# Eleven pairs of expert tiles by seven block products in the second half of V

## The chip, the cores and the metric

The kernel runs on one core of a Trainium2 chip. The metric is the device time of one launch in microseconds. A core has TensorE for matmuls, VectorE, ScalarE and GpSimd for elementwise work, and DMA queues; here SyncE (SP) issues nearly all transfers.

## The reference

Two transformer blocks on 256 tokens of width 2048, all in float32. The change touches the last matmul only. After the second block's attention, each token chooses experts out of 16384. With `u` and `v` the tables of the chosen experts:

```python
a = jax.nn.gelu(jnp.einsum('thkd,td->thk', u, xb).astype(jnp.float32), approximate=False)
coef = (g * a).astype(xb.dtype)
return jnp.einsum('thk,thkd->td', coef, v_emb[expert])
```

The result is added to `x`, and an RMS norm with the gain `norm_final_g` gives the output.

## The kernel before

All experts are computed densely. `G[expert, token]` (128 expert tiles of 128, by 256 tokens) holds the coefficients, zero where a token didn't choose an expert, and the V stage computes `G`-transposed times V (16384 by 2048). It runs in two halves of 1024 columns, c = 0 and c = 1. In each half, tile j adds for two token halves (qt) and two column blocks of 512 (b) a product of 128 x 128 by 128 x 512 to one of four PSUM banks (`acc`, line 832). Float32 accuracy is kept with two parts of each operand, a high part rounded to fp32r and the low rest, so each product is three matmuls (`three`, lines 940 to 943: high by high, high by low, low by high). A tile is 12 matmuls.

`PLAN` is the list of all weight chunks in order of use (512 KB each here), `AT` its inverse, `NCH` its length. Each engine runs its own program in that order:

- SP loads chunk i to one of RN = 4 places of `raw` (`load`, line 838), once VectorE is done with chunk i - 4 (semaphore `lo`). What stands in front of a load on SP holds it back.
- ScalarE casts chunk i to `wh` (line 2273), after its load has landed (`d_w`) and after TensorE finished chunk i - SN, SN = 3 (`gemm`). VectorE writes `wl` = `raw` - `wh` (line 1481) and signals `lo`.
- `coef_high(n)` (line 2655, ScalarE) and `coef_low(n)` (line 2189, VectorE, semaphore `c_l`) do the same for the coefficients of tile n mod 128, in two places used by turns. `coef_high(n)` waits until TensorE finished tile n - 2.
- In the loops over j for the second half, ScalarE and VectorE do the coefficients of tile j + 1 and then the weights of tile j + 2. ScalarE's turn j starts when TensorE has finished tile j - 1.
- TensorE (`v_tile`) waits for `lo` and `c_l` of its tile.

Around this: the residual (`spill`, 8 pieces of 256 KB) and the final gain (4 pieces) are read back into `G`'s own space while the second half runs. `PIECE` says at which chunk, and each piece n waits on SP for `c_l` >= 128 + 2n + 2, since it overwrites the coefficients of used tiles. `ADD_AT` says in which turns VectorE adds the first half's four PSUM banks to the residual. ScalarE squares the sums with an accumulated row sum, and VectorE multiplies by the gain, a little later. The last three tiles are ordered by bank (`v_last`), so that the final norm can begin early. GpSimd has no work after the placing of the weights in the table.

```python
PIECE = {AT["V", 10 + 2 * n, 1]: n for n in range(12)}
ADD_AT = [50 + 4 * n for n in range(4)]
```

Of the kernel before, what the change touches and what calls it, by code (L numbers as in the profile page):

```python
# [7 lines left out]
F32 = mybir.dt.float32  # L8
# [8 lines left out]
D = 2048  # L17
# [143 lines left out]
PLAN += [("V", j, c) for c in range(2) for j in range(128)]  # L161
# [7 lines left out]
PIECE = {AT["V", 10 + 2 * n, 1]: n for n in range(12)}  # L169

ADD_AT = [50 + 4 * n for n in range(4)]
# [323 lines left out]
def build(nc, A, out):  # L495
# [184 lines left out]
    fin = flatG[:, 0:2 * D].rearrange("p (q d) -> p q d", q=2)  # L680
# [26 lines left out]
    def pc(name, i=0):  # L707
# [53 lines left out]
        new(n) for n in ("v_part", "f_add", "f_sq", "f_ms", "f_rt", "f_rs", "f_out", "f_outv")]  # L761
    block = top.enter_context(nc.Block())
# [74 lines left out]
    def _(y):  # L837
# [42 lines left out]
        for i in range(RN, NCH):  # L880
# [30 lines left out]
            if i in PIECE:  # L911
                n = PIECE[i]
                if n == 0:
                    y.wait_ge(d_spill, 16)
                y.wait_ge(c_l, 128 + 2 * n + 2)
                c = slice(512 * (n % 4), 512 * (n % 4) + 512)
                if n < 8:
                    y.dma_start(fin[:, n // 4, c], spill[:, n // 4, c]).then_inc(d_re, 16)
                else:
                    y.dma_start(gain[:, c], A["g_final"][:, c]).then_inc(d_gf, 16)  # L920
            load(i)
# [6 lines left out]
        for qt in range(2):  # L928
            for n in range(2):
                for sem, c in ((f_out, 512 * n), (f_outv, CH + 512 * n)):  # L930
                    if (qt, n, sem) == (1, 1, f_out):
                        continue
                    y.wait_ge(sem, 2 * qt + n + 1)
                    y.dma_start(out[128 * qt:128 * qt + 128, c:c + 512], fin[:, qt, c:c + 512]).then_inc(d_out, 16)
# [4 lines left out]
    def _(t):  # L939
# [495 lines left out]

        def v_last():
# [16 lines left out]
        for i in range(U0, NCH):  # L1453
            name, j, c = PLAN[i]
            if name == "U":
                if c == 0:
                    if j < 4:
                        t.wait_ge(qp_ok, 5 + j)
                    else:
                        t.wait_ge(ev_u, j - 3)  # L1460
                chunk(i, u_place(j), 8 * c, 8, x4, c == 0, c == 1)
            elif (j, c) == (125, 1):
                v_last()
            elif c == 0 or j < 125:
                v_tile(j, c)
# [6 lines left out]
    def _(v):  # L1472
# [731 lines left out]
        def add_up(half, qt, b):  # L2204
            i = 2 * half + b
            x = fin[:, qt, 512 * i:512 * i + 512]
            v.tensor_tensor(x, x, acc(half, qt, b)[:], ALU.add).then_inc(f_add, 1)

        for j in range(128):
            if j < 125:  # L2210
                coef_low(128 + j + 1)
# [11 lines left out]
            else:  # L2223
                cut(V1 + j + 2)
            if j in ADD_AT:
                n = ADD_AT.index(j)
                if n == 0:
                    v.wait_ge(d_re, 16 * 8)
                add_up(0, n // 2, n % 2)
            if j - 2 in ADD_AT:  # L2230
                n = ADD_AT.index(j - 2)
                if n == 0:
                    v.wait_ge(d_gf, 16 * 4)
                x = fin[:, n // 2, 512 * (n % 2):512 * (n % 2) + 512]
                v.wait_ge(f_sq, n + 1)
                v.tensor_tensor(x, x, gain[:, 512 * (n % 2):512 * (n % 2) + 512], ALU.mult).then_inc(own.up(), 1)
        for qt in range(2):
            for b in range(2):
# [6 lines left out]
                else:  # L2245
                    for c in (0, 256):
                        x = fin[:, 1, 1536 + c:1792 + c]
# [9 lines left out]
            for c in (CH, CH + 512):  # L2257
                y = fin[:, qt, c:c + 512]
# [4 lines left out]
    def _(s):  # L2263
# [404 lines left out]
        def square_up(half, qt, b):  # L2668
            i, n = 2 * half + b, 4 * half + 2 * qt + b
            s.wait_ge(f_add, n + 1)  # L2670
            s.activation(squares[:, qt, 512 * i:512 * i + 512], fin[:, qt, 512 * i:512 * i + 512], ACT.Square,
                         accum_out=ssum[:, qt, i:i + 1]).then_inc(f_sq, 1)

        for j in range(128):
            if j < 126:
                coef_high(128 + j + 1)
# [8 lines left out]
            else:  # L2685
                cut(AT["V", j, 1] + 2)
            if j - 1 in ADD_AT:
                n = ADD_AT.index(j - 1)
                square_up(0, n // 2, n % 2)
        for qt in range(2):  # L2690
# [4 lines left out]
            else:  # L2695
                for n, c in ((0, 1536), (1, 1792)):
                    s.wait_ge(f_add, 8 + n)
                    s.activation(squares[:, 1, c:c + 256], fin[:, 1, c:c + 256], ACT.Square,
# [14 lines left out]
    def _(g):  # L2713
# [91 lines left out]
        put(1, 7)  # L2805

# [118 lines left out]
```

## Time and profile before

| What | Value |
| --- | --- |
| median of 3 runs | 3174.89 us (3174.85 to 3175.99) |
| profiled execution | 3175.95 us, of it 3174.1 us span |
| mean granted TensorE clock | 0.999 |
| TensorE matmuls | 24186 |
| second half of V | about 2812 to 3161 us |

The span runs from the first to the last instruction. "Busy" of TensorE counts pipelined matmuls: one lasts 0.39 us in the records but the next begins 0.23 us after it, so the pitch, not the duration, gives its cost. A line of the profile names line, engine, operation, output and inputs. The tile `coefs` is the pair of coefficient buffers, and `G` also stands for everything laid over its space.

### The profile page before, as it was taken

What the parts mean: (1) busy time and instruction counts of PE and PEld (TensorE: products, weight loads), DVE (VectorE), ACT (ScalarE), POOL (GpSimd) and SP (SyncE); (2) the same over time, 40 slices, a digit from 0 to 9 for tenths busy, and PEclk for the clock granted to TensorE, in tenths of its full rate; (3) what the DMA queues carried; (4) which work ended last, traced back from release to release, by engine and by line L of the source; (5) the groups of instructions that cost most, each with busy time, mean ns of one, the idle gap of its engine ahead of it and who ended that gap; (6) DMA issues with size and microseconds to landing.
All of it is one profiled execution on the core that took longest, in us unless ns stands there. A gap on an engine that the chain in (4) does not pass through costs nothing.

```text
span 3174.1 us, 58774 instructions
## 1 busy us (share of the span) xinstructions
PE 3160.3 (100%) x24186; PEld 3018.3 (95%) x24186; DVE 2096.0 (66%) x3389; ACT 1804.0 (57%) x2580; POOL 458.0 (14%) x321
## 2 busy tenths in 40 slices
PE   9999999999999999999999999999999999999998
PEld 9999999999999999999999999999999888888887
DVE  7987486666664477665666699855555666666665
ACT  6566464444444455545455578877777544555545
POOL 0001200000000000000000056777760000000000
PEclk9999999999999999999999999999999999999999
DMA  6444557666666656545565577888876777766555
GB/s 224 151 146 134 183 181 235 225 226 229 226 201 194 194 172 206 163 153 166 187 196 197 199 190 194 196 195 195 194 195 196 243 242 242 242 226 216 195 194 168
DMA packets 229419, 627.77 MB, mean 198 GB/s; under 512 B 59328, under 2 KB 78624, under 8 KB 229024
## 3 DMA queue, kind: packets, MB, share of 16 engines
q1 hardware_dynamic: 192144, 623.60, 60.7%
q0 software_dynamic: 36864, 0.15, 3.3%
q8 instruction: 192, 3.15, 0.4%
q14 instruction: 75, 0.61, 0.1%
q10 hardware_dynamic: 144, 0.26, 0.0%
HBM read 601.27 MB, written 21.10 MB: 196 GB/s over the span
## 4 chain that ended last, share of the span: by engine, by line
PE 98%; DVE 1%; ACT 0%; DMA 0%; issue 0%; POOL 0%; SPq 0%; DVEq 0%; ACTq 0%; POOLq 0%
PE ps L941 32%; PE ps L942 31%; PE ps L943 31%; PE ps L1014 0%; DVE wl L1481 0%; PE ps L1215 0%; PE ps L1238 0%; PE ps L1235 0%; PE ps L982 0%; DMA raw<-in_in1k 0%; PE ps L1411 0%; PE ps L1249 0%; PE ps L1239 0%; PE ps L1067 0%; PE ps L1016 0%
## 5 line engine op out<-in xcount | busy, mean ns | idle before, releaser
L2273 ACT CAST wh<-raw 128x1024 fp32r<-128x1024 f32 (+3 forms) x1114 | 1158.2, 1040 | 1029.7 <-PE ps L943 1008.4
L1481 DVE TENSOR_TENSOR wl<-raw,wh 128x1024 fp32r<-128x1024 f32 (+2 forms) x883 | 1061.8, 1203 | 407.8 <-ACT wh L2273 405.4
L941 PE MATMUL ps<-xh,wh 128*128 128x256 f32 x3088 | 854.7, 277 | 0.5 <-issue 0.5
L943 PE MATMUL ps<-xh,wl 128*128 128x256 f32 x3088 | 850.0, 275 | 0.0
L942 PE MATMUL ps<-xl,wh 128*128 128x256 f32 x3088 | 849.8, 275 | 0.0
L941 PE MATMUL ps<-xw,wh 128*128 128x258 f32 (+2 forms) x2096 | 591.7, 282 | 2.8 <-DVE wl L1542 1.7
L943 PE MATMUL ps<-xw,wl 128*128 128x258 f32 (+2 forms) x2096 | 587.6, 280 | 0.0
L941 PEld LDWEIGHTS ps<-xh,wh 128*128 128x128 f32 x3088 | 579.7, 188 | 4.3 <-issue 1.6
L942 PEld LDWEIGHTS ps<-xl,wh 128*128 128x128 f32 x3088 | 579.8, 188 | 1.1 <-issue 1.0
L943 PEld LDWEIGHTS ps<-xh,wl 128*128 128x128 f32 x3088 | 579.6, 188 | 0.0
L2784 POOL DMA_INDIRECT table<-w_loose x256 | 397.6, 1553 | 809.3 <-DVE w_loose L2161 656.3
L1481 DVE TENSOR_TENSOR wl<-raw,ph 128x1024 fp32r<-128x1024 f32 x231 | 281.2, 1220 | 224.4 <-ACT ph L2278 187.7
L942 PE MATMUL ps<-xw,wh 128*128 128x258 f32 (+2 forms) x1441 | 404.2, 281 | 0.0
L941 PEld LDWEIGHTS ps<-xw,wh 128*128 128x128 f32 x2096 | 394.3, 188 | 5.4 <-DVE wl L1542 2.1
L943 PE MATMUL ps<-wh,coefs 128*128 128x512 f32 x1020 | 396.8, 389 | 0.0
L941 PE MATMUL ps<-wh,coefs 128*128 128x512 f32 x1020 | 396.8, 389 | 0.0
L942 PE MATMUL ps<-wl,coefs 128*128 128x512 f32 x1020 | 396.8, 389 | 0.0
L943 PEld LDWEIGHTS ps<-xw,wl 128*128 128x128 f32 x2096 | 394.0, 188 | 0.0
L942 PEld LDWEIGHTS ps<-xw,wh 128*128 128x128 f32 x1441 | 270.8, 188 | 0.1
L2278 ACT CAST ph<-raw 128x1024 fp32r<-128x1024 f32 x231 | 232.7, 1007 | 0.0
L941 PEld LDWEIGHTS ps<-wh,coefs 128*128 128x128 f32 x1020 | 191.4, 188 | 39.8
L943 PEld LDWEIGHTS ps<-wh,coefs 128*128 128x128 f32 x1020 | 191.4, 188 | 39.8
(398 smaller groups left out, 4454.7 us busy)
## 6 DMA issues: line engine op xcount, KB each, us to landing
raw<-in_peer_u SPq DMA_DIRECT2D x256, 512.0 KB
raw<-in_peer_v SPq DMA_DIRECT2D x256, 512.0 KB
raw<-in_w_in SPq DMA_DIRECT2D x172, 512.0 KB
raw<-in_w_up SPq DMA_DIRECT2D x82, 512.0 KB
raw<-in_w_gate SPq DMA_DIRECT2D x80, 512.0 KB
raw<-in_w_down SPq DMA_DIRECT2D x80, 512.0 KB
raw<-in_w_out SPq DMA_DIRECT2D x64, 512.0 KB
table<-tmp SPq DMA_DIRECT2D x32, 512.0 KB, 6.4
```

Of the source, the lines that this page charges most:

```text
L941: t.matmul(o, lh, rh, start=start, stop=False)
L942: t.matmul(o, lh, rl, start=False, stop=False)
L943: return t.matmul(o, ll, rh, start=False, stop=stop)
L1481: v.tensor_tensor(part_at(wl, i), raw[:, i % RN, 0:cols(i)], high.bitcast(F32), ALU.subtract).then_inc(lo, 1)
L2273: last = s.copy(part_at(wh, i), raw[:, i % RN, 0:cols(i)])
L2278: last = s.copy(ph[:, 2 + i % 2, :], raw[:, i % RN, 0:cols(i)])
L2784: g.indirect_dma_start(out=table, out_offset=bass.IndirectOffsetOnAxis(ap=eidx[q][:, n:n + 1], axis=0), in_=wts[q][:, n:n + 1], in_offset= ...
```

## The change

Eleven pairs of neighbouring tiles (26 and 27, 34 and 35, ..., 106 and 107) leave the ordinary order of the second half. For such a pair the eight block products (two tiles, two token halves, two column blocks) are replaced by seven, in the manner of Strassen and Winograd, with four sums of weight blocks (T1 to T4) and four sums of coefficient blocks.

- TensorE: `v_pair(n)` runs ahead of the tile behind the pair, 7 x 3 matmuls. Three products go to the banks of the second half, four to the banks `ps[4]` to `ps[7]` of the first half, which are kept over all pairs.
- SP: the pair's raw weights (2 x 512 KB) go to a place of their own in `G`'s space (`PAIR_LOAD`). They stand ahead of the load of the chunk eight places behind the first single tile of the stretch, and wait for the fourth of the previous pair's five subtractions (`pair_lo`).
- GpSimd: `pair_sums`, 4 subtractions of 512 columns and 4 ops of 128 columns a pair, after TensorE has finished the previous pair (the sums lie where the low parts will).
- ScalarE and VectorE: `pair_step`, the cast and the subtraction of the pair's 4096 columns in five parts, one a turn in the six turns between two pairs, behind the turn's own work (VectorE one turn after ScalarE).
- Behind the last pair VectorE folds the four extra banks into the residual (`FOLD`, eight ops in turns 109 to 116), ScalarE copies one bank.
- `PIECE`, `ADD_AT`, the squares and the gains move: residual pieces 0 to 3 to tiles 8 to 14, 4 to 7 to tiles 109 to 112, the gain to tiles 18 to 24; the waits for `c_l` stay as they were.

```diff
-PLAN += [("V", j, c) for c in range(2) for j in range(128)]
+PAIRS = [26 + 8 * n for n in range(11)]
+PAIRED = [j + e for j in PAIRS for e in range(2)]
+SINGLE = [j for j in range(128) if j not in PAIRED]
+PLAN += [("V", j, 0) for j in range(128)] + [("V", j, 1) for j in SINGLE]
...
-PIECE = {AT["V", 10 + 2 * n, 1]: n for n in range(12)}
-
-ADD_AT = [50 + 4 * n for n in range(4)]
+PIECE = {AT["V", j, 1]: n for n, j in enumerate((8, 10, 12, 14, 109, 110, 111, 112, 18, 20, 22, 24))}
+
+ADD_AT = [11, 12, 13, 14]
+SQUARE_AT, GAIN_AT = [48, 56, 64, 72], [49, 57, 65, 73]
...
+BETWEEN = PAIRS[1] - PAIRS[0] - 2
+PAIR_LOAD = {AT["V", 20, 1]: 0}
+PAIR_LOAD.update({AT["V", j - BETWEEN, 1] + 8: n + 1 for n, j in enumerate(PAIRS[:-1])})
+BEHIND_PAIR = {j - BETWEEN + o: (n, o) for n, j in enumerate(PAIRS) for o in range(BETWEEN)}
+FOLD = {PAIRS[-1] + 3 + n: n for n in range(8)}
...
                 y.wait_ge(c_l, 128 + 2 * n + 2)
                 c = slice(512 * (n % 4), 512 * (n % 4) + 512)
+                if n == 4:
+                    y.wait_ge(pair_lo, PAIR_LO + 5 * (len(PAIRS) - 1) + 4)
...
+            if i in PAIR_LOAD:
+                n = PAIR_LOAD[i]
+                if n:
+                    y.wait_ge(pair_lo, PAIR_LO + 5 * (n - 1) + 4)
+                else:
+                    y.wait_ge(c_l, 128 + 16)
+                for e in range(2):
+                    j = PAIRS[n] + e
+                    y.dma_start(flatG[:, (2 + e) * CH:(3 + e) * CH], A["peer_v_2"][128 * j:128 * j + 128, CH:2 * CH]).then_inc(d_pair, 16)
             load(i)
...
+            if first:
+                t.wait_ge(f_add, 4)
+            t.wait_ge(pair_lo, PAIR_LO + 5 * (n + 1))
+            t.wait_ge(c_l, one + 1)
+            product(ps[4], single(one, 0), B11, first, last)
+            product(ps[5], summed(0), T1_, first, last)
+            t.wait_ge(c_l, two + 1)
+            product(acc(1, 0, 0), single(two, 0), B21, False, False)
+            product(acc(1, 1, 0), single(two, 1), T4_, False, False).then_inc(pair_mm, 1)
+            product(acc(1, 0, 1), summed(3), B22, False, False)
+            product(ps[6], summed(1), T2_, first, last)
+            product(ps[7], summed(2), T3_, first, last).then_inc(pair_mm, 1)
...
+        def pair_step(n, o):
+            if 1 <= o < 6:
+                pair_low_of(n, o - 1)
+
+        def pair_low_of(n, q):
+            x, y = ((0, 512), (512, 1536), (1536, 2560), (2560, 3584), (3584, 4096))[q]
+            whole_ = RAW11 if q == 0 else RAW_ROWS if q == 1 else pair_raw[:, x:y]
+            v.wait_ge(pair_hi, PAIR_HI + 5 * n + q + 1)
+            v.tensor_tensor(pair_low[:, x:y], whole_, pair_high[:, x:y].bitcast(F32), ALU.subtract).then_inc(pair_lo, 1)
...
+            if j in PAIRS:
+                coef_low(128 + j + 1)
+                cut(AT["V", j + 2, 1] + 2)
+                continue
...
+            elif n >= 130 and n - 130 in PAIRED:
+                s.wait_ge(pair_mm, PAIR_MM + 2 * (PAIRED.index(n - 130) // 2) + 1)
...
+            if o == 0:
+                if n:
+                    s.wait_ge(pair_mm, PAIR_MM + 2 * n)
+                s.wait_ge(d_pair, D_PAIR + 32 * (n + 1))
+            elif o > 1:
+                s.wait_ge(pair_sum, PAIR_SUM + 8 * n + (3, 4, 8)[o - 2])
+            s.copy(pair_high[:, x:y], whole_).then_inc(pair_hi, 1)
...
+            if n:
+                g.wait_ge(pair_mm, PAIR_MM + 2 * n)
+            g.wait_ge(d_pair, D_PAIR + 32 * (n + 1))
+            g.tensor_tensor(t1, RAW12, RAW11, ALU.subtract).then_inc(pair_sum, 1)
+            g.tensor_tensor(t3, RAW22, RAW12, ALU.subtract).then_inc(pair_sum, 1)
```

## Rows read from the trace of the kernel before

**Rows 1.** The page: engine, busy us, share of the span, instructions.

```profile
PE 3160.3 (100%) x24186; PEld 3018.3 (95%) x24186; DVE 2096.0 (66%) x3389; ACT 1804.0 (57%) x2580; POOL 458.0 (14%) x321
```

**Rows 2.** The page: the chain that ended last, by engine.

```profile
PE 98%; DVE 1%; ACT 0%; DMA 0%; issue 0%; POOL 0%; SPq 0%; DVEq 0%; ACTq 0%; POOLq 0%
```

**Rows 3.** Waits, 2812 to 3160: who waited for whom; total us, times, longest.

```profile
ACT coefs L2655 <- PE ps L943: 168.3, 126, 1.4
DVE wl L1481 <- ACT wh L2273: 66.1, 125, 0.6
```

**Rows 4.** Timeline of one tile: start, duration, engine, line, operation [idle before it].

```profile
2841.90 0.39 PE L941 MATMUL ps<-wh,coefs 128*128 128x512 f32 x1
...
2842.10 0.41 ACT L2655 CAST coefs<-G 128x256 fp32r<-128x256 f32 x1 [1.36 <-PE ps L943]
...
2842.41 1.05 ACT L2273 CAST wh<-raw 128x1024 fp32r<-128x1024 f32 x1
2842.54 0.42 DVE L2189 TENSOR_TENSOR coefs<-G,coefs 128x256 fp32r<-128x256 f32 x1 [0.54 <-ACT coefs L2655]
...
2843.50 1.22 DVE L1481 TENSOR_TENSOR wl<-raw,wh 128x1024 fp32r<-128x1024 f32 x1 [0.53 <-ACT wh L2273]
...
2844.62 0.39 PE L941 MATMUL ps<-wh,coefs 128*128 128x512 f32 x1
```

**Rows 5.** Timeline, VectorE in the first half of V, ops back to back.

```profile
2802.74 0.42 DVE L2189 TENSOR_TENSOR coefs<-G,coefs 128x256 fp32r<-128x256 f32 x1 [0.82 <-ACT coefs L2655]
2803.09 1.22 DVE L1481 TENSOR_TENSOR wl<-raw,wh 128x1024 fp32r<-128x1024 f32 x1
2804.22 0.42 DVE L2185 TENSOR_TENSOR G<-G,tmp 128x256 f32<-128x256 f32 x1
```

**Rows 6.** Groups by form, 2812 to 3160: VectorE on 512 columns.

```profile
L2220 DVE TENSOR_TENSOR wl<-raw,wh 128x512 fp32r<-128x512 f32 x2 | 1.3, 687 | 0.1
```

**Rows 7.** Timeline of SP's queue, 2839 to 2845: start, duration of the issue.

```profile
2839.31 0.33 SPq L842 DMA_DIRECT2D raw<-in_peer_v  x1
2839.68 0.43 SPq L918 DMA_DIRECT2D G<-spill  x1
```

**Rows 8.** DMA issues (whole run; last line 2850 to 3160): count, KB, us to landing.

```profile
spill<-G SPq DMA_DIRECT2D x1, 2048.0 KB, 7.8
...
par<-in_par SPq DMA_DIRECT2D x1, 8.0 KB, 1.7
...
G<-spill SPq DMA_DIRECT2D x4, 256.0 KB, 5.4
```

**Rows 9.** Windows: us, busy of PE, PEld, DVE, ACT, POOL; clock, DMA share, GB/s.

```profile
3165.00:3166.00 1.00, 0.94 (x5) 0.42 (x3) 1.00 (x2) 0.50 (x2) 0.00 (x0) 1.00 0.31 119
3166.00:3167.00 1.00, 0.00 (x0) 0.00 (x0) 0.74 (x3) 0.88 (x3) 0.00 (x0) 1.00 1.03 387
3168.00:3169.00 1.00, 0.00 (x0) 0.00 (x0) 0.70 (x3) 0.72 (x2) 0.00 (x0) 0.66 0.55 191
3169.00:3170.00 1.00, 0.00 (x0) 0.00 (x0) 0.90 (x2) 0.82 (x2) 0.00 (x0) 0.50 0.00 0
```

**Rows 10.** Timelines of GpSimd beside VectorE; last, line 1648: min/median/max ns.

```profile
931.34 0.74 POOL L2721 TENSOR_TENSOR tmp<-tmp 128x256 f32<-128x256 f32 x1 [481.18 <-ACT tmp L2437]
...
114.74 1.21 DVE L1481 TENSOR_TENSOR wl<-raw,wh 128x1024 fp32r<-128x1024 f32 x1
114.90 1.65 POOL L2759 TENSOR_TENSOR csum<-cacc 128x258 f32<-128x258 f32 x1 [88.48 <-DVE cacc L1692]
...
115.87 0.71 DVE L1648 SCALAR_TENSOR_TENSOR pexp<-pexp,stat 16x16 f32<-16x16 f32 x1
...
L1648 DVE SCALAR_TENSOR_TENSOR pexp<-pexp,stat x12: 217/350/706, 115.9 to 184.8; 16x16 f32<-16x16 f32 x4, 128x144 f32<-128x144 f32 x4, 128x272 f32<-128x272 f32 x4
```

More of the change, by code:

```diff
@@ L1434, in v_tile, with v_pair, product, single @@
             last.then_inc(gemm, 1)
+        def v_pair(n):
+            j = PAIRS[n]
+            one, two = 128 + j, 128 + j + 1
+            first, last = n == 0, n == len(PAIRS) - 1
+            def product(o, left, b, start, stop):
+                return three(o[:], *left, pair_block(pair_high, b), pair_block(pair_low, b), start, stop)
+            def single(tile, qt):
+                tk = slice(128 * qt, 128 * qt + 128)
+                return coef_at(0, tile)[:, tk], coef_at(1, tile)[:, tk]
+            def summed(i):
+                return pair_sum_at(pair_high, i), pair_sum_at(pair_low, i)
+            if first:
[10 more added lines that the diff above has]
+            product(ps[7], summed(2), T3_, first, last).then_inc(pair_mm, 1)
         def v_last():
@@ L1464, in _ @@
             elif c == 0 or j < 125:
+                if c and j - 2 in PAIRS:
+                    v_pair(PAIRS.index(j - 2))
                 v_tile(j, c)
@@ L2222, in _ @@
                 last.then_inc(lo, 1)
-            else:
-                cut(V1 + j + 2)
+            elif j in SINGLE and j - 2 not in PAIRS:
+                cut(AT["V", j, 1] + 2)
+            if j in BEHIND_PAIR:
+                pair_step(*BEHIND_PAIR[j])
+            if j in FOLD:
+                fold(FOLD[j])
             if j in ADD_AT:
@@ L2684, in _ @@
                 s.copy(part_at(wh, i)[:, 512:CH], raw[:, i % RN, 512:CH]).then_inc(hi, 1)
-            else:
+            elif j in SINGLE and j - 2 not in PAIRS:
                 cut(AT["V", j, 1] + 2)
-            if j - 1 in ADD_AT:
-                n = ADD_AT.index(j - 1)
+            if j in BEHIND_PAIR:
+                pair_step(*BEHIND_PAIR[j])
+            if j == PAIRS[-1] + 2:
+                s.wait_ge(pair_mm, PAIR_MM + 2 * len(PAIRS))
+                s.copy(folded, ps[6][:]).then_inc(pair_hi, 1)
+            if j in SQUARE_AT:
+                n = SQUARE_AT.index(j)
                 square_up(0, n // 2, n % 2)
@@ L2805, in _, with pair_sums @@
         put(1, 7)
+        def pair_sums(n):
+            j = PAIRS[n]
+            g.wait_ge(coef, j + 2)
+            g.wait_ge(c_l, 128 + 16)
+            a11, a21, a12, a22 = [G[:, j + e, 128 * qt:128 * qt + 128] for e in range(2) for qt in range(2)]
+            t1, t2, t3, t4 = [pair_block(pair_raw, b) for b in (T1_, T2_, T3_, T4_)]
+            sums = [pair_sum_at(pair_raw, i) for i in range(4)]
+            done = PAIR_SUM + 8 * n
+            if n:
[3 more added lines that the diff above has]
+            g.tensor_tensor(t3, RAW22, RAW12, ALU.subtract).then_inc(pair_sum, 1)
+            g.wait_ge(pair_sum, done + 1)
+            g.tensor_tensor(t2, RAW22, t1, ALU.subtract).then_inc(pair_sum, 1)
+            g.wait_ge(pair_sum, done + 3)
+            g.tensor_tensor(t4, RAW21, t2, ALU.subtract).then_inc(pair_sum, 1)
+            g.tensor_tensor(sums[0], a21, a22, ALU.add).then_inc(pair_sum, 1)
+            g.tensor_tensor(sums[2], a11, a21, ALU.subtract).then_inc(pair_sum, 1)
+            g.wait_ge(pair_sum, done + 5)
+            g.tensor_tensor(sums[1], sums[0], a11, ALU.subtract).then_inc(pair_sum, 1)
+            g.wait_ge(pair_sum, done + 7)
+            g.tensor_tensor(sums[3], a12, sums[1], ALU.subtract).then_inc(pair_sum, 1)
+        for n in range(len(PAIRS)):
+            pair_sums(n)
     px.close()
```

62 lines of the change are left out of this document (48 added, 14 removed).

## The prediction

> **What bounds the kernel now.** I read the page from the top: TensorE is busy for the whole span, VectorE and ScalarE for two thirds or less [rows 1]. The chain of waits says the same: 98% of the path that ended last is TensorE [rows 2]. So the time is the number of matmuls times their pitch, plus each pause in them. The changed stage is the second half of V (about 2812 to 3160 us). Its waits show that the other engines wait for TensorE: ScalarE 168 us at the coefficients, VectorE 66 us for ScalarE [rows 3]; TensorE waits for nobody. One tile tells the schedule [rows 4]: its first matmul starts at 2841.90, the next tile's at 2844.62, so a tile is 2.72 us for 12 matmuls of 512 columns, 0.227 each. I call a tile's start S. In loop turn j ScalarE casts the coefficients of tile j+1 at S+0.20 and the weights of tile j+2 at S+0.51; VectorE subtracts the coefficients at S+0.64 to 1.06 and the weights at S+1.60 to 2.82. The coefficients are 1.66 us ahead of their use, the weights 2.6 us. Both engines work through their queue in order: a wait in front of one cast holds everything behind it.
>
> Busy ops follow each other faster than they last [rows 5]: VectorE 1.13 us for 1024 columns, 0.35 for 256. 512 columns last 0.69 us [rows 6]; for their pitch I take 0.60.
>
> **What is saved.** A pair of tiles has 8 block products of 3 matmuls, now 7: 3 x 0.227 = 0.68 us a pair, 7.5 us for eleven. That is 0.24% and the most the change can bring. U, the first half of V and the tail stay.
>
> **Added work.** Per pair ScalarE and VectorE each go over 4096 columns instead of 2048. VectorE in turn j of a working tile: 0.35 + 1.13 + 1.13 = 2.6 us of 2.72. It fits, but only just, and it comes late: the pair's subtraction stands behind the tile's, at S+2.73 to 3.96. The eight folds (j = 109 to 116) and the moved additions, squares and gains are one short op in a turn that has at least 0.4 us left: nothing, the tile's 2.72 us cover them.
>
> **Pair start.** The last of the five subtractions (512 columns of sums) is in turn PAIRS-1, after the weights: 2.73 to 3.42 after S, while TensorE wants it at 2.72. `v_pair` waits for all five, so it starts 0.70 us late, 0.75 with the wake-up. What is queued behind is all of TensorE. This alone eats the 0.68. Where GpSimd has delayed VectorE before (below), it is up to 1.7, most of one GpSimd op more. I take 1.0, near the lower end, since only the last turns count (bounds 0.75 and 1.7; not below, because VectorE's own queue makes the 0.75).
>
> **Pair loads on SP's queue.** `PAIR_LOAD` for pair n+1 stands in front of the load of the fifth single tile behind pair n's beginning: for pair 26 it is tile 30. SP first waits for the fourth subtraction of pair n (call its end W: turn 24, S+3.96, that is 1.5 us before the pair is due), then issues 2 x 512 KB, and only then the 512 KB of tile 30. ScalarE wants tile 30 in turn 26, as the pair begins, ahead of the cast of tile 28's coefficients. How long do 1536 KB take? No row has it. SP's issues are 0.37 us apart [rows 7]. A 256 KB piece issued 0.37 behind a 512 KB load lands after 5.4 us, so 768 KB after 5.8 from the first issue; the 2048 KB spill takes 7.8 [rows 8]. Between them on a straight line: 1536 KB 7.0 us, 1792 KB 7.4. Lower bound: the 1.7 us of the 8 KB transfer [rows 8] plus the bytes at the 387 GB/s that the engines moved at the end [rows 9]: 5.8 us, and 3.7 for 768 KB, 6.4 for 1792. I take the line, because it lies between two landings of this very queue.
> So tile 30 lands at W+7.05. The pair starts at W+2.25 and ends at W+2.25+21 x 0.227 = W+7.0. From a landing to the next tile's first matmul: ScalarE's cast 1.05, VectorE's subtraction 1.13, then the coefficients 0.42, wake-ups 0.2: 2.8 us. TensorE stands for about 2.85 us behind each pair but the last.
>
> **GpSimd's sums.** They wait for the pair's end, so GpSimd starts just then. Alone, 256 columns took 0.74 us; behind a subtraction of VectorE (114.74 to 115.95) 1.65 us, 0.60 after that ended; and VectorE's next op, a 16x16 one of 0.22 at least, took 0.71 [rows 10]. So the two take turns, and a waiting GpSimd gets its turn between two VectorE ops. For 512 columns I take a little over twice the 0.60: 1.25 us. One such op ahead of the subtraction (which hides about 0.5 of it) or one between it and the coefficients adds 0 to 2.0 us to the 2.85. I take 1.25, one op in the way: 4.1 in all (bounds 2.85 and 4.85).
> The Trainium skill ("SBUF — State Buffer", Who interferes with whom) states this as an exclusive lock between a VectorE op with two SBUF inputs and a GpSimd op, held for the whole instruction; the rows agree (1.65 against 0.74). It speaks against "GpSimd makes the sums" being free. Without it the sum would be 12 us lower.
> Per pair: -0.68 + 1.0 + 4.1 = +4.4; ten pairs +44 us.
>
> **Last pair.** No pair load follows, but piece 4 (in front of tile 109) waits for the same fourth subtraction, then 256 KB, then tile 109: 768 KB from 1.5 before the due start, so landing 4.35 after it. ScalarE wants it in turn 105, and VectorE's last subtraction for the pair stands behind it: 1.05 + 1.13 + 0.69 + 0.1. The pair starts 7.3 us late. -0.68 + 7.3 = +6.6.
>
> **Moved pieces of the gain.** Pieces 8 to 11 move from tiles 26 to 32 to tiles 18 to 24, but their wait (c_l >= 146, 148, 150, 152) is unchanged: it is met in turns 16, 18, 20, 22. The load of tile 18 is behind it on SP, and ScalarE wants tile 18 in turn 16. Before, the same wait was long met. Tile 18: 1.1 (coefficients of turn 16) + 5.8 + 2.8 = 9.7 for the 5.44 of two tiles: +4.3. Tile 20: the wait is met 1.45 after tile 18's start; pair 0's 1024 KB go ahead too, 7.4; +2.8 = 11.65: +6.2. Tile 22: 1.45 + 5.8 + 2.8: +4.6. Tile 24: pair 0's subtractions add 0.6 before and 1.1 behind, 11.75: +6.3. Sum +21.4 us; with the fast transfers 7.3 less, +14.1.
>
> **Sum.** 21.4 + 44 + 6.6 = +72.0 us on the profiled execution's 3175.95: 3248; it is 1.06 above the median of the runs, so 3247.
> The Trainium skill ("DMA: Bandwidth & Descriptors", Anatomy of one DMA) fits one transfer with about 2.0 us plus bytes over 436 GB/s: 5.6 us for 1536 KB, 3.8 for 768. By that estimate the sum would be 23 us lower. The rows for queued transfers (5.4 and 7.8) are slower, and no row has one load alone.
>
> **Rivals.**
> A, fast transfers: landings by the lower bound. Pieces 14.1, pair waits 2.85 - 1.2 = 1.65 with GpSimd hidden: ten pairs x 2.0 = 20, the last 6.6 - 2.1 = 4.5: +38.6, so 3214 - 1 = 3213. With the 0.75 at the pair starts too it is 3211. For it: 387 GB/s in the end's row. Against it: both landings of SP's queue.
> B, TensorE's clock falls in the pauses. TensorE ended at about 3165.9; the granted clock was 1.00 until 3167, 0.66 in the mean of 3168 to 3169 and 0.50 (the 1.2 GHz level) after that [rows 9]. The fifteen pauses forecast here are 4 to 7 us long. No row shows it coming back; if each pause costs one tile at the half level, that is 2.72 more, so 0 to 41 us on top. The middle of that gives 3268. The Trainium skill ("TensorE: Matmul & The Clock Gate", Part 1) says that activity releases the throttle again, so it would be a price per pause. Against it: later stalls shrink while TensorE is slow.
> C, the other side, faster: the preparation never binds and only the 7 products count. Then 3174.9 - 7.5 = 3167.4. It decides where the fourth subtraction is over 5 us earlier, or the queue delivers 1536 KB in under 4 us, and where the 0.70 of the last subtraction vanishes; the first two I see nowhere.
> D, only the pair start binds (SP's waits are met early): -7.5 + 11 x 0.85 = +2, 3177. For it: SP's queue is empty when it wakes. Against it: the 5.8 us.
> E, the change doesn't do what it says: a pair in fact keeps its eighth product and the time stays. `v_pair` lists seven, so I give it nothing.
>
> **How the numbers follow.** Forecast with its own spread 0.50, A 0.20, B 0.20, C 0.04, D 0.06. Range 3205 to 3285: the low end is A less one microsecond at every second pause, the high end B with most of its price. A measurement tells 0.2% (6.3 us) from no change. Faster: C, 0.04. Same: D, 0.06. Slower: 0.90.
>
> **What would show it.** Matmuls down by 33. TensorE waiting for VectorE's coefficient subtraction at tiles 18, 20, 22, 24 (4 to 6 us each) and at the tile behind each pair (about 4), with ScalarE's weight cast waiting for the DMA `raw`; a wait of 0.7 to 1.7 at each pair start, over 7 before the last. GpSimd's 512-column ops 1.2 us alone and 2 to 2.5 behind VectorE. If ScalarE's cast never waits for `raw`, the sum is wrong from its base, and it is C or D. If the granted clock drops under 1 in the stage, B.

## The result: 3276.4 us, 3.2% slower, and the profile after

The changed kernel takes 3276.43 us in the median of 4 runs (3274.3 to 3278.46), the kernel before 3174.88. The ratio is 1.0319, with a 95% interval of 1.0301 to 1.0337. The time is 29 us above the forecast of 3247 and inside its range of 3205 to 3285.

The page of the kernel after: busy us of each engine, the granted clock in 40 slices of the span (9 is 90% or more), and the chain that ended last.

```profile
span 3274.2 us, 58871 instructions
...
PE 3192.3 (97%) x24153; PEld 3030.7 (93%) x24153; DVE 2148.7 (66%) x3430; ACT 1824.6 (56%) x2614; POOL 548.0 (17%) x409
...
PEclk9999999999999999999999999999999999989899
...
PE 91%; DVE 4%; DMA 3%; ACT 1%; issue 0%; SPq 0%; POOL 0%; DVEq 0%; ACTq 0%; POOLq 0%
```

The 33 matmuls are saved (24186 before [rows 1]). But the chain, 98% TensorE before [rows 2], now has 4% of VectorE and 3% of DMA in it, and the clock has dents in the last slices. The waits of the second half of V (2808 to 3262; us in total, times, longest), beside [rows 3]:

```profile
ACT coefs L2758 <- PE ps L984: 159.1, 96, 7.9
DVE wl L1552 <- ACT wh L2374: 116.0, 69, 8.9
ACT wh L2374 <- DMA raw<-in_peer_v: 87.7, 16, 9.3
...
PE ps L982 <- DVE coefs L2260: 56.2, 14, 6.2
```

Two lines are new: ScalarE's weight cast waits 16 times for a load, and TensorE 14 times for coefficients. Fourteen is four pieces of the gain and ten pairs.

**A piece of the gain** (timeline: start, duration, engine, line [idle before]; tile 18 was due at about 2865.5):

```profile
2861.14 0.33 SPq L952 DMA_DIRECT2D G<-in_g_final  x1
...
2861.51 0.91 SPq L871 DMA_DIRECT2D raw<-in_peer_v  x2
...
2867.17 1.04 ACT L2374 CAST wh<-raw 128x1024 fp32r<-128x1024 f32 x1 [6.51 <-DMA raw<-in_peer_v]
2868.12 0.40 ACT L2758 CAST coefs<-G 128x256 fp32r<-128x256 f32 x1
2868.24 1.22 DVE L1552 TENSOR_TENSOR wl<-raw,wh 128x1024 fp32r<-128x1024 f32 x1 [7.13 <-ACT wh L2374]
...
2869.95 0.77 PE L982 MATMUL ps<-wh,coefs 128*128 128x512 f32 x1 [4.30 <-DVE coefs L2260]
```

The piece is issued at 2861.14, the tile's load behind it, and the cast begins at 2867.17: 6.0 us for 768 KB, forecast 5.8. From there to the matmul it is 2.78, forecast 2.8.

**Behind a pair** (timeline; the pair's last matmul is the first line):

```profile
3028.70 0.39 PE L984 MATMUL ps<-xh,xl 128*128 128x512 f32 x1
3029.33 1.27 POOL L2943 TENSOR_TENSOR x_loose<-G 128x512 f32<-128x512 f32 x1 [20.27 <-PE ps L984]
3029.84 1.83 DVE L1552 TENSOR_TENSOR wl<-raw,wh 128x1024 fp32r<-128x1024 f32 x1 [4.99 <-ACT wh L2374]
3030.55 2.24 POOL L2944 TENSOR_TENSOR x_loose<-G 128x512 f32<-128x512 f32 x1
3031.60 2.89 DVE L2260 TENSOR_TENSOR coefs<-G,coefs 128x256 fp32r<-128x256 f32 x2
...
3033.22 0.76 PE L982 MATMUL ps<-wh,coefs 128*128 128x512 f32 x1 [4.13 <-DVE coefs L2260]
```

VectorE's subtraction, 1.22 us alone, lasts 1.83 behind GpSimd's first op; GpSimd's second, 1.27 alone, lasts 2.24 behind VectorE; the two subtractions of coefficients take 2.89 with a GpSimd op between them, 0.42 each alone [rows 4].

**Where the 101 us are.** I took the start of every 512-column matmul from the timeline and sorted the distances to the next one against 0.2267 us, the spacing of before [rows 4]. Over 0.35 us too long is a pause; 0.1 to 0.35 too long is a slow matmul; the rest is spacing. In after there are 140 slow ones, 114 of them 0.42 to 0.43 us apart. From "all three mended" on, the clock is 1.00 in the whole stage, so there the column holds short waits and no slow clock. Against it stand the 33 matmuls that are gone, 7.5 us. The last column is the time of the profiled execution less the before of its chip (3174.8 to 3175.2). The kernels below the first line are those of the experiments.

| kernel | pauses | slow matmuls | longer spacing | saved | sum | measured |
| --- | --- | --- | --- | --- | --- | --- |
| after | 73.3 | 27.8 | 7.5 | -7.5 | 101.1 | 101.1 |
| gain's pieces later | 59.9 | 23.9 | 5.4 | -7.5 | 81.7 | 82.2 |
| pair load later | 37.7 | 13.0 | 8.5 | -7.5 | 51.7 | 52.6 |
| GpSimd later | 57.8 | 24.3 | 7.9 | -7.5 | 82.5 | 82.5 |
| fillers, short | 74.1 | 14.6 | 7.2 | -7.5 | 88.4 | 88.0 |
| fillers, long | 76.8 | 4.1 | 8.4 | -7.5 | 81.8 | 82.0 |
| all three mended | 12.6 | 4.3 | 8.6 | -7.5 | 18.0 | 18.4 |
| and the sums first | 2.7 | 4.5 | 9.7 | -7.5 | 9.4 | 10.0 |
| mended, thin sums | 7.6 | 1.1 | 7.7 | -7.5 | 8.9 | 9.3 |
| before, one wait added | 1.2 | 0.0 | 8.9 | 0 | 10.1 | 9.6 |
| thin sums, sums first | 0.0 | 0.5 | 7.7 | -7.5 | 0.7 | 0.6 |
| VectorE makes the sums | 0.4 | 0.6 | 8.0 | -7.5 | 1.5 | 2.3 |
| and products in halves | 0.0 | 0.8 | 8.7 | -7.5 | 2.0 | 1.4 |

The sum closes to within 1 us in every kernel, so three things, and no fourth, have to be explained: pauses (forecast), slow matmuls (a rival), and a longer spacing (in nobody's forecast).

The slow matmuls are TensorE's clock. Windows of after (us; busy of PE, PEld, DVE, ACT, POOL; granted clock, DMA share, GB/s) over a pause that ends at 2946.50:

```profile
2944.00:2946.50 2.50, 0.00 (x0) 0.03 (x1) 2.50 (x3) 0.00 (x0) 2.50 (x2) 1.00 0.60 234
...
2946.50:2948.00 1.50, 1.50 (x5) 1.21 (x6) 1.27 (x1) 0.00 (x0) 1.42 (x2) 0.67 0.75 273
2948.00:2950.00 2.00, 2.00 (x6) 1.58 (x5) 0.00 (x0) 0.00 (x0) 2.00 (x4) 0.50 0.03 10
2950.00:2951.00 1.00, 1.00 (x5) 0.79 (x4) 0.00 (x0) 0.00 (x0) 0.60 (x2) 0.78 0.00 0
2951.00:2952.00 1.00, 1.00 (x6) 0.82 (x5) 0.42 (x1) 0.88 (x2) 0.00 (x0) 1.00 0.00 0
```

In this pause the clock is still 1.00. It falls to 0.50, the 1.2 GHz level, when TensorE works again, and is back at 1.00 by 2951. Elsewhere it falls within the pause, as in the one above that ends at 3033.22:

```profile
3032.40:3033.20 0.80, 0.00 (x0) 0.01 (x1) 0.80 (x2) 0.00 (x0) 0.80 (x2) 0.50 0.37 113
```

It fell thirteen times in the stage, nine times within a pause and four times up to 0.9 us behind one. Either way it stays low for some microseconds in which TensorE works again, so the price of a pause is paid by the matmuls behind it.

### The profile page after: what moved, and what is told of

The parts are those of the page before. It is cut to its first block, busy times and chain, and to the rows that moved or that the text cites. A ratio compares the mean times of both kernels' runs of the same rounds, so it can differ in the third digit from the quotient of the medians.

```text
span 3274.2 us, 58871 instructions
## 1 busy us (share of the span) xinstructions
PE 3192.3 (97%) x24153; PEld 3030.7 (93%) x24153; DVE 2148.7 (66%) x3430; ACT 1824.6 (56%) x2614; POOL 548.0 (17%) x409
## 4 chain that ended last, share of the span: by engine, by line
PE 91%; DVE 4%; DMA 3%; ACT 1%; issue 0%; SPq 0%; POOL 0%; DVEq 0%; ACTq 0%; POOLq 0%
PE ps L982 29%; PE ps L983 29%; PE ps L984 29%; DMA raw<-in_peer_v 3%; DVE wl L1552 2%; ACT wh L2374 1%; DVE xl L2288 1%; DVE coefs L2260 1%; PE ps L1055 0%; SPq L961 0%; DMA raw<-in_in1k 0%; PE ps L1256 0%; PE ps L1276 0%; PE ps L1279 0%; PE ps L1023 0%
## 5 line engine op out<-in xcount | busy, mean ns | idle before, releaser
L2374 ACT CAST wh<-raw 128x1024 fp32r<-128x1024 f32 (+3 forms) x1092 | 1134.8, 1039 | 1116.7 <-PE ps L984 1009.1
L1552 DVE TENSOR_TENSOR wl<-raw,wh 128x1024 fp32r<-128x1024 f32 (+2 forms) x861 | 1042.5, 1212 | 457.5 <-ACT wh L2374 452.6
L982 PE MATMUL ps<-wh,coefs 128*128 128x512 f32 x932 | 376.6, 404 | 56.2 <-DVE coefs L2260 56.2
L983 PE MATMUL ps<-wl,coefs 128*128 128x512 f32 x932 | 374.6, 402 | 0.0
L984 PE MATMUL ps<-wh,coefs 128*128 128x512 f32 x932 | 374.1, 401 | 0.0
L982 PEld LDWEIGHTS ps<-wh,coefs 128*128 128x128 f32 x932 | 181.8, 195 | 101.2 <-issue 54.0
L2260 DVE TENSOR_TENSOR coefs<-G,coefs 128x256 fp32r<-128x256 f32 x254 | 128.7, 510 | 166.2 <-ACT coefs L2758 165.8
```

What stands on the lines that cost most here:

```text
L982: t.matmul(o, lh, rh, start=start, stop=False)
L983: t.matmul(o, lh, rl, start=False, stop=False)
L984: return t.matmul(o, ll, rh, start=False, stop=stop)
L1552: v.tensor_tensor(part_at(wl, i), raw[:, i % RN, 0:cols(i)], high.bitcast(F32), ALU.subtract).then_inc(lo, 1)
L2260: v.tensor_tensor(coef_at(1, n), G[:, n % 128, :], coef_at(0, n).bitcast(F32), ALU.subtract).then_inc(c_l, 1)
L2374: last = s.copy(part_at(wh, i), raw[:, i % RN, 0:cols(i)])
```

## The experiments

Each changes the kernel after, unless it says otherwise. The pauses and spacings are from the same list of starts. The first three kernels and the two with fillers were measured once each, the others 4 to 11 times. The repeated ones spread by 1 to 2 us, and after by 4, so a miss of 3 us in a kernel measured once says little.

### The gain's pieces at later tiles

```diff
-PIECE = {... (8, 10, 12, 14, 109, 110, 111, 112, 18, 20, 22, 24)}
+PIECE = {... (8, 10, 12, 14, 109, 110, 111, 112, 29, 31, 32, 33)}
```

> The changed kernel with one thing undone: the four pieces of the gain are loaded in front of tiles 29, 31, 32 and 33 instead of 18, 20, 22 and 24, where their wait is long met. My theory (the loads of tiles 18 to 24 stand behind a wait that is met only in the turn that needs them): the pauses of 4.46, 5.06, 1.73 and 6.36 us vanish, and with them the half clock behind three of them, 2 to 3 us each: 17.6 + 8 less, so 3276 becomes 3248 to 3254. Rival (the pauses come from the first GpSimd sums and the 1024 KB of pair 0, not from the pieces' wait): at most the 1 or 2 us at tile 20 go, over 3270.

Measured 3257.42 beside 3175.2: 19 us better than after, 3 us above the range expected. The pauses at tiles 18, 20, 22 and 24 (4.46, 5.06, 1.73 and 6.36 us) are gone. In their place the pause behind pair 0 grows from 0.91 to 4.30 us, like those behind the others. So the pieces cost 17.6 us of pauses, of which 3.4 return, and the slow matmuls fall by 4, from 27.8 to 23.9.

### The pair's load two chunks later

```diff
-PAIR_LOAD.update({AT["V", j - BETWEEN, 1] + 8: n + 1 ...
+PAIR_LOAD.update({AT["V", j - BETWEEN, 1] + 10: n + 1 ...
```

> The changed kernel with one number changed: the raw weights of the next pair are issued two chunks later in SP's order (in front of tile 32 where it was tile 30), so that tiles 30 and 31 are loaded before SP waits for the fourth subtraction. The pair's weights are issued at nearly the same moment. My theory (the pause behind a pair is tile 30 arriving late): the nine pauses of about 4.3 us behind the pairs, 40 us in all, go to under 1 us each, and with them 2 to 3 us of half clock each; 3276 becomes 3210 to 3225. ScalarE's weight cast no longer waits for raw there. Rival (the pause is GpSimd taking VectorE's port right behind the pair): 1.25 to 2.5 us of each pause stay, without half clock, and the result is 3228 to 3240.

Measured 3227.84: 48.6 us less than after, from one number, and 3 us above the range expected; the rival's 3228 to 3240 begins at its edge. Its waits (2812 to 3215):

```profile
ACT wh L2374 <- DMA raw<-in_peer_v: 40.7, 6, 9.8
...
PEld ps L982 <- DVE xl L2288: 21.2, 10, 8.1
```

ScalarE waits for 6 loads instead of 16, and all pauses behind pairs are gone, though GpSimd's sums are where they were. Every pair now starts 1.18 us late instead of 0.68 (0.79 the first, 7.79 the last). That these 0.5 a pair are GpSimd's price is not shown here, but below, where its sums are cut to 4 columns and the starts are 0.68 late again. Of the 35.6 us fewer pauses, 40.8 come from behind the pairs and 5 go back at the starts; another 14.8 come from the clock.

### GpSimd's sums two tiles later

```diff
                 g.wait_ge(pair_mm, PAIR_MM + 2 * n)
+                g.wait_ge(c_l, 128 + PAIRS[n - 1] + 4)
```

> The changed kernel with GpSimd's sums held back until VectorE has done the coefficients of both tiles behind the pair. My theory (4.1 us behind a pair are 2.85 us of late load plus one GpSimd op in the way): the pauses behind the pairs fall from 4.3 to about 3.0, 9 x 1.3 = 12 us, and a microsecond of half clock with some of them: 3258 to 3266. Rival (GpSimd is hidden behind the late load, the pause is the load alone): no change, over 3272; or the sums come too late for ScalarE and the pair starts grow by more than is saved: slower than 3276.

Measured 3257.73, just under the range expected. The ten pauses behind pairs sum to 25.4 us instead of 40.8. With the load late, GpSimd adds 1.5 us a pair (forecast 1.25), and the late load alone leaves 2.5 (forecast 2.85). With the load in time it adds 0.5 (1.18 for 0.68 at the starts, above). The two causes are not additive: GpSimd's turns cost the most where VectorE is already the last to be waited for.

### Fillers in the pauses, short and long

Matmuls of a 128 x 128 block of ones are added into a bank of the second half in each pause, so that TensorE doesn't stand idle (and the output isn't the reference's). Short: 11 behind a piece, 10 behind a pair, 18 before the last. Long: 18, 18 and 28.

```diff
+        def fill(n):
+            for _ in range(n):
+                t.matmul(acc(1, 0, 0)[:, 0:128], ones[:], ones[:], start=False, stop=False)
```

> The changed kernel with float32 matmuls of ones put where TensorE pauses: 11 in front of tiles 18, 20, 22 and 24, 10 behind each pair but the last, 18 in front of the last pair (0.37 us each by the first rows of the trace). They add ones to one PSUM bank, so the output is not the reference's; nothing else is changed. If the granted clock is a cost of its own, as my rival B says, it stays at 1.00 and the slow matmuls go (28 us in the profile), while the pauses stay in length: 3276 becomes 3240 to 3252. If the slow matmuls only fill time that the preparation would take anyway, it stays at 3270 or more.

> The changed kernel, again with float32 matmuls of ones in TensorE's pauses, but more of them, since they took 0.24 us each in e6_fill and so filled only half: 18 in front of tiles 18 to 24 and behind each pair but the last, 28 in front of the last pair. They add ones to one PSUM bank, so the output is not the reference's. If the half clock is a price of its own, the granted clock stays at 1.00 except perhaps behind the two longest pauses, the slow matmuls nearly vanish and the time falls to 3238 to 3252. If the clock is no cost, it stays at the 3263 of e6_fill or above.

Measured 3263.17 and 3256.78, the mean clock 0.994 and 0.998 (after: 0.988). Both lie above their ranges. One filler took 0.23 us (35 records, 4.07 us, two to a filler, the line below), so that the ten behind a pair, 2.3 us, filled half of a pause. In the second, the slow matmuls' excess falls from 27.8 to 4.1 us, while the pauses grow by 3.5. The fillers behind a pair, and the windows there, where after was at 0.50:

```profile
2946.29 4.07 PE L1479 MATMUL ps<-ones 128*128 128x128 f32 x35
```

```profile
2940.00:2946.00 6.00, 5.49 (x25) 4.14 (x24) 1.59 (x3) 1.01 (x2) 0.00 (x0) 1.00 0.95 347
2946.00:2952.00 6.00, 6.00 (x46) 5.64 (x45) 4.04 (x3) 1.58 (x4) 5.35 (x4) 1.00 0.74 263
```

So with the clock held up about 24 us of slow matmuls are gone, and 19 us of the time. The difference is mostly pauses: behind pair 0 the 4.07 us of fillers are longer than the 0.91 us that TensorE paused there before. The slow clock is the term that the forecast left out.

### All three pauses mended

The two edits above, and the residual's last pieces and the folds four tiles later.

```diff
-PIECE = {... (8, 10, 12, 14, 109, 110, 111, 112, 18, 20, 22, 24)}
+PIECE = {... (8, 10, 12, 14, 112, 113, 114, 115, 29, 31, 32, 33)}
-FOLD = {PAIRS[-1] + 3 + n: n for n in range(8)}
+FOLD = {PAIRS[-1] + 7 + n: n for n in range(8)}
```

> All three waits on SP's queue moved at once: the gain's pieces in front of tiles 29 to 33, the next pair's weights two chunks later, and the residual's pieces 4 to 7 in front of tiles 112 to 115 with the folds four turns later. Nothing else differs from the changed kernel. My theory (SP's queue order is the whole loss but for the pair starts): no pause over 2 us is left, the clock stays at 1.00, and what remains is eleven pair starts of 0.7 to 1.2 us against 7.5 us saved: 3174 to 3182. Rival (the seven products have other costs of their own, such as GpSimd's sums): over 3190.

Measured 3192.96 (3192.18 to 3193.26), ratio 1.0055 (1.0039 to 1.0072): 83.5 us better than after, but 11 above the range, and slower than before. The last pause of 7 us is gone; ten pair starts of 1.19 are what is left of pauses, 0.72 the first. The rest was first unexplained: 12.6 of pauses less 7.5 saved is 5, not 18. The list of starts showed it: the spacing is 0.2333 us instead of 0.2267 nearly everywhere from 2868.6 until 3176, a moment before the end of the stage. It changes where TensorE was first held up, by 0.2 us. There GpSimd makes the sums of pair 0, which take turns with VectorE's coefficients (1.17 and 1.51 us instead of 0.42) and weights (2.31 instead of 1.22):

```profile
2864.49 1.47 POOL L2944 TENSOR_TENSOR x_loose<-G 128x512 f32<-128x512 f32 x1
2864.73 2.31 DVE L1552 TENSOR_TENSOR wl<-raw,wh 128x1024 fp32r<-128x1024 f32 x1
2865.92 2.27 POOL L2946 TENSOR_TENSOR x_loose<-G,x_loose 128x512 f32<-128x512 f32 x1
2866.97 1.51 DVE L2260 TENSOR_TENSOR coefs<-G,coefs 128x256 fp32r<-128x256 f32 x1
...
2868.21 0.39 PE L984 MATMUL ps<-wh,coefs 128*128 128x512 f32 x1
2868.62 0.47 PE L982 MATMUL ps<-wh,coefs 128*128 128x512 f32 x1
```

### The pair's sums ahead of the weights

As the kernel before this one, with all three pauses mended; and in the turn before a pair, VectorE subtracts the sums first and the tile's weights behind them.

```diff
+                ahead = j in BEHIND_PAIR and BEHIND_PAIR[j][1] == 5
+                if ahead:
+                    pair_step(*BEHIND_PAIR[j])
                 if j in SINGLE and j - 2 not in PAIRS:
                     cut(AT["V", j, 1] + 2)
```

> The kernel e4_all with one more change: in the last turn before a pair, VectorE subtracts the pair's 512 columns of sums ahead of the tile's weights and no longer behind them. My theory (the pair start waits for the last op in VectorE's queue): the pair starts cost under 0.2 us, so 8 to 13 us less than e4_all, 3167 to 3171, faster than the kernel before. Rival (GpSimd has pushed VectorE back by more than that op): the pause at the pair start stays at 0.5 us or more, 3174 or more.

Measured 3184.7 (3183.75 to 3185.75), ratio 1.003 (1.0019 to 1.0042): 14 us above the range. The pauses at the starts are gone, as expected (12.6 to 2.7 us; the 2.7 are five pauses of 0.4 to 0.6, four of them within a pair, where TensorE waits for the second tile's coefficients). The time stays 10 us above before: 9.7 of spacing, 2.7 of pauses and 4.5 of short waits, less the 7.5 saved.

### GpSimd's sums cut to 4 columns

All three pauses mended, and each of GpSimd's eight ops works on 4 columns only. The kernel then multiplies other data: the casts of the sums read raw rows in their place.

```diff
-            t1, t2, t3, t4 = [pair_block(pair_raw, b) for b in (T1_, T2_, T3_, T4_)]
+            t1, t2, t3, t4 = [pair_block(pair_raw, b)[:, 0:4] for b in (T1_, T2_, T3_, T4_)]
```

> The kernel e4_all with GpSimd's sums cut to 4 columns each, and ScalarE and VectorE taking the parts that held the sums from raw weights and coefficients already there; all other instructions, sizes and waits are the same. The sums are missing, so the output is not the reference's. My theory (GpSimd holds VectorE up by about half a microsecond a pair, the rest of the pair start is VectorE's own queue): the pair starts are 0.7 us instead of 1.2, so 4 to 6 us less than e4_all. Rival (GpSimd's ops all find free time once the loads come in time): within 1.5 us of e4_all.

Measured 3184.47 (3183.13 to 3185.03): 8.5 less than with the whole sums, more than the 4 to 6 expected. The pair starts are 0.67 to 0.68 us late instead of 1.19, which is the forecast's 0.75 to within a tenth; 5 us less are there, 3 in the small waits, 1 in the spacing.

### The kernel before with one wait added

No pair, nothing moved. Once, at tile 18, TensorE also waits for the next tile's coefficients.

```diff
+            if n == 146:
+                t.wait_ge(c_l, n + 2)
```

> The kernel before, without any pair. Its single edit: at tile 18 of the second half of V TensorE waits for the coefficients of the tile behind it as well, one wait of about 1.1 us, once. Theory (in the kernels with pairs a 512-column matmul of this stage takes 0.233 us instead of 0.227 at full clock from the first moment at which TensorE or its weight load has to wait, and it stays so): +1.1 us, and then about 110 tiles x 13 matmuls x 0.0066 us = 9 us: 3184 to 3186. Rival (the longer spacing belongs to the pairs, to GpSimd's sums or to their transfers): +1.1 us alone, 3175.5 to 3176.5, spacing 0.227 behind the wait as before it.

Measured 3184.76 (3184.52 to 3185.34), ratio 1.003 (1.0018 to 1.0041), inside the theory's range of 3184 to 3186. The wait of 1.04 us, and the starts behind it:

```profile
2865.08 0.39 PE L943 MATMUL ps<-wh,coefs 128*128 128x512 f32 x1
...
2866.51 0.47 PE L941 MATMUL ps<-wh,coefs 128*128 128x512 f32 x1 [1.04 <-DVE coefs L2191]
```

Windows from 2870 to 3150, first the kernel before, then this one:

```profile
2870.00:3150.00 280.00, 280.00 (x1237) 231.85 (x1236) 174.22 (x215) 142.60 (x215) 0.00 (x0) 1.00 0.60 198
```

```profile
2870.00:3150.00 280.00, 280.00 (x1202) 226.75 (x1201) 169.99 (x208) 138.31 (x209) 0.00 (x0) 1.00 0.58 191
```

Both are busy for all of the 280 us at a clock of 1.00 without any wait, yet the second gets 1202 matmuls done and the first 1237. 280 / 1202 is 0.233 us, 280 / 1237 is 0.226. One wait of a microsecond in a stage without waits has cost 9.6.

### Thin sums, and the sums first

All three pauses mended, with the thin sums and the sums first.

```diff
-            t1, t2, t3, t4 = [pair_block(pair_raw, b) for b in (T1_, T2_, T3_, T4_)]
+            t1, t2, t3, t4 = [pair_block(pair_raw, b)[:, 0:4] for b in (T1_, T2_, T3_, T4_)]
...
+                if ahead:
+                    pair_step(*BEHIND_PAIR[j])
```

> As e9_all_thin (all the pauses mended, GpSimd's sums of 4 columns each, so that the kernel computes another result), and besides the subtraction of each pair's sums stands ahead of its tile's weights in the turn before, as in e5_all_first. If the longer spacing comes from a first wait of TensorE and nothing else, and no wait is left, the spacing stays at 0.227 us and the time is the saving of the record: 3167 to 3170. If a small wait within the pair is left (the second tile's coefficients), the spacing changes there: 3176 to 3181. If the spacing belongs to the pairs' other data (three operands per matmul group, the transfers), the same 3176 to 3181, but the change lies at a place where TensorE did not wait.

Measured 3175.67 (3175.01 to 3176.62), ratio 1.0001 (0.9992 to 1.0011). TensorE has no pause left, the saving of 7.5 us is there, and the spacing takes 7.7 of it. Here it changes in the first pair, within its first product: the distances behind the first two matmuls below are 0.227 and 0.231, and the next one is 0.232. Single distances in the pair scatter, and from the next tile on it is 0.233.

```profile
2887.34 0.39 PE L982 MATMUL ps<-xh,coefs 128*128 128x512 f32 x1
2887.56 0.39 PE L983 MATMUL ps<-xl,coefs 128*128 128x512 f32 x1
2887.79 0.40 PE L984 MATMUL ps<-xh,coefs 128*128 128x512 f32 x1
2888.03 0.39 PE L982 MATMUL ps<-xh 128*128 128x512 f32 x1
2888.26 0.39 PE L983 MATMUL ps<-xl,xh 128*128 128x512 f32 x1
```

No wait is recorded there. By the expectation's three outcomes this is the last, a change where TensorE did not wait, though the time lies below the 3176 that stood beside it. So a wait is enough to lengthen the spacing, but none that the profile records is needed.

### VectorE makes the sums

As the kernel with the sums first, with the eight ops on VectorE, four in each of two turns, and none on GpSimd.

```diff
+            if o == 0:
+                pair_sums(n, 0)
...
+            if o == 1:
+                pair_sums(n, 1)
...
-        for n in range(len(PAIRS)):
-            pair_sums(n)
```

> As e5_all_first (all the pauses mended, sums ahead of the weights), but VectorE makes the eight sums and differences of a pair, four in each of the two steps that lie ahead of it, and GpSimd none. The sums of GpSimd took 1.3 to 1.8 us each of 512 columns and held VectorE up; VectorE's own should take about 0.6 each, so that VectorE and GpSimd together lose 6 to 8 us per pair less. Theory that GpSimd's sums cost the rest: no waits at the pairs, 3167 to 3177, the upper end if one wait of TensorE still lengthens the spacing. Rival (VectorE's queue becomes the bound with 2.4 us more in each of two steps): waits of 0.5 to 2 us per pair, 3185 to 3200.

Measured 3176.8 (3175.54 to 3177.71), ratio 1.0005 (0.9995 to 1.0015), at the upper end of the theory's range. VectorE and GpSimd by operation, 2812 to 3160 (count, busy us, mean ns), first after's GpSimd, then this kernel's VectorE:

```profile
L2944 POOL TENSOR_TENSOR x_loose<-G 128x512 f32<-128x512 f32 x10 | 17.9, 1794 | 0.0
```

```profile
L2291 DVE TENSOR_TENSOR x_loose<-G 128x512 f32<-128x512 f32 x11 | 7.5, 685 | 0.0
```

The same op takes VectorE 0.69 us; GpSimd took 1.79 and held VectorE up besides. VectorE makes the sums in its idle time and TensorE keeps 0.4 us of pauses. This is the whole change without its pauses, and with the right result: it is as fast as the kernel before, no faster.

### Products in halves

As the one before, and the first of the four products of each single tile from 18 on is six matmuls of 256 columns instead of three of 512.

```diff
+            if half and a == 0 and 18 <= j < 125:
+                for c in (0, 256):
+                    last = three(acc(half, qt, b)[:, c:c + 256], coef_at(0, n)[:, tk], coef_at(1, n)[:, tk],
```

> As e13_dve (3176.8), and in each single tile of the second half of V from tile 18 on the first of its four products is issued as six matmuls of 256 columns instead of three of 512: the same arithmetic, three instructions more per tile. In the kernel before the matmuls of 256 columns come back to 0.1133 us, half of 0.2267, after every disturbance. Theory that the longer spacing is a state that only matmuls of 512 columns keep, and that shorter ones put right: behind each split the spacing is 0.227 again, all but the tiles with a wait within them run at it, 85 tiles x 9 matmuls x 0.0066 us = 5 us and the halves themselves another 1.7 less: 3169 to 3172. Rival 1 (the state outlives them): the halves at 0.1133 and the rest at 0.233: 3175 to 3177. Rival 2 (the halves take over their weights too late and cost more than half a matmul each): 3178 to 3195.

Measured 3176.85 (3176.4 to 3177.92), ratio 1.0006 (0.9997 to 1.0015): rival 1. The starts:

```profile
2898.14 0.28 PE L982 MATMUL ps<-wh,coefs 128*128 128x256 f32 x1
2898.26 0.28 PE L983 MATMUL ps<-wl,coefs 128*128 128x256 f32 x1
2898.37 0.28 PE L984 MATMUL ps<-wh,coefs 128*128 128x256 f32 x1
...
2898.85 0.40 PE L982 MATMUL ps<-wh,coefs 128*128 128x512 f32 x1
2899.09 0.40 PE L983 MATMUL ps<-wl,coefs 128*128 128x512 f32 x1
2899.32 0.39 PE L984 MATMUL ps<-wh,coefs 128*128 128x512 f32 x1
```

The halves themselves are 0.118 us apart, not the 0.1133 of the earlier stages, and the matmuls behind them 0.233. Shorter matmuls don't put the spacing right, and are lengthened with it.

## Why the prediction was right, and 29 us low

Direction, cause and places of the pauses were right; one rival was under-weighted; one term was missing.

- **Saving, 7.5.** 24186 - 24153 = 33 matmuls of 0.2267: right.
- **Landings.** 768 KB forecast 5.8: 6.0 at tile 18 (issue 2861.14 to cast 2867.17), 5.8 at the last pair (3194.75 to 3200.54). The straight line between two landings of the queue was right, and rival A (3.7 us) wrong. The Trainium skill ("DMA: Bandwidth & Descriptors", Anatomy of one DMA), from which the prediction had 3.8 us, states its fit for the path through GpSimd, while SyncE issues these transfers; no run here has one of this size alone.
- **Moved pieces, 21.4.** Measured 4.46, 5.06, 1.73 and 6.36, together 17.6, for 4.3, 6.2, 4.6 and 6.3. The mis-sized one is tile 22. I had taken each pause alone, though TensorE ran at half clock behind tile 20's and so gave the preparation room. The slow matmuls ahead of tile 22 are 2.9 us too long, and 2.9 + 1.7 is the 4.6 of the forecast. In the kernel with GpSimd's sums later they are 1.5 too long there and the pause is 4.0. Both fit this reason, but no run changes the clock there and nothing else.
- **Pause behind a pair, 4.1 each, 41 for ten.** Measured 4.29 or 4.30 six times, 5.52 and 5.53, 3.11, and 0.91 behind the first: 40.8. The split was 2.5 and 1.5 a pair instead of 2.85 and 1.25, so that the sum of 4.1 was met because two errors cancel. The 2.85 also goes with a start 0.75 late; with the 1.0 that the sum takes for the start it is 2.6.
- **Pair start, 1.0 each.** Measured 0.67 to 0.68 for seven, 0.75 to 0.96 for three: the lower bound of 0.75 was the right value. 7.3 us instead of 10. My reason for going higher, GpSimd's delays, holds only with the load in time (1.18).
- **Last pair, 7.3.** Measured 7.18.
- Together the pauses were forecast at 79.7 us (21.4 + 41 + 10 + 7.3) and are 73.3. Without the clock and the spacing the time would be 3174.9 + 73.3 - 7.5 = 3240.7, 6 under the forecast. Those 6 us hide a part of the 35 (27.8 and 7.5) that the sum lacked: that the miss is 29 and no more is luck.
- **Rival B, the clock, 0 to 41, middle 20.5.** Measured 27.8 us of slow matmuls, and the long fillers took 23.7 of it away. The failed step is the weighing: "No row shows it coming back" made me leave it out of the sum, though [rows 9] show it falling between 1 and 3 us after the end of the matmuls, and fifteen pauses of that length were my own forecast. A price bounded by 0 on one side and 41 on the other should have stood in the sum at its middle. The Trainium skill ("TensorE: Matmul & The Clock Gate", Wait — 56ns, not 53.3ns?) has N / 1.2 GHz, 427 ns, for the throttled distance of 512 columns; the trace agrees, 0.43 us.
- **No term for the spacing, 7.5.** "Number of matmuls times their pitch" took the pitch as fixed. It has a second level 2.9% higher, and the stage went over to it at the first disturbance.
- **C, faster (3167.4).** Ruled out for a reason that no part of the forecast had. Even with every pause gone the time is 3175.7 to 3176.8, since 8 us of spacing eat the 7.5 saved. The change as such is worth nothing here. What it cost, 101 us, are its pauses and the slow clock behind them.

The Trainium skill's exclusive lock ("SBUF — State Buffer", Who interferes with whom) is borne out by the lengthened ops behind the pair. The sum had 12 us for it. By the experiments GpSimd's sums cost 15 us of pauses with the load late and 5 with it in time.

## What the runs showed of the hardware that I had not expected

**Two spacings at full clock.** A 512-column matmul of this stage starts 0.2267 us after the last one, or 0.2333, at a granted clock of 1.00 and without a recorded wait in either. The lower one holds for the whole stage of the kernel before until 3159. The higher one sets in with a first hold-up of 0.2 or 1.2 us, or within a pair without one, and lasts: in the kernel with one wait added, for 300 us, to the end. Behind matmuls at half clock it sometimes went back, in after from 2982 to 2994, and with the gain's pieces later from 3191 to 3239. In the last three tiles, whose products come in another order, it changes without a recorded wait and in either direction: up in the kernel before at 3159, down in the one with all three pauses mended at 3176. The Trainium skill ("TensorE: Matmul & The Clock Gate", Back-to-back issue gap) gives 216 ns for an isolated 512-column matmul and 131 sustained; the trace has 227 and 233 here. What the state is, what in a pair's products brings it about, and what ends it, stays open.

**The clock falls late in a pause or just behind it.** In after it fell 3.0 to 4.8 us after the next matmul was due. So some pauses of 4.3 us have the clock at 1.00 throughout, others at 0.50 in their last microsecond, and either kind has matmuls at half clock behind it.

**A 128-column float32 filler takes 0.23 us** in two records (18 fillers in 4.07 us), as much as a 512-column fp32r matmul of the kernel.

## What to carry to other kernels

In a stage that TensorE bounds with no wait at all, count what a change puts in front of a load on an in-order DMA queue, and when the wait ahead of it is met: here one number (the pair's load two chunks later) was worth 49 of 101 us. Price pauses like those here, of 3 to 7 us, at more than their length: 73 us of pauses came with 27.8 us of slow matmuls and 7.5 of longer spacing, though the spacing came in one kernel without any pause as well. And before a saving of 0.24% is built, disturb the kernel once on purpose: the 9.6 us that one short wait cost here were more than the saving.
